# Input projections of the last mixers as three single-pass products over half weight items

## The reference

```
h = rms_norm_2(x, norm1_g) * (1.0 + sc1) + sh1
hc = rms_norm_2(ctx, norm1_g) * (1.0 + csc1) + csh1
mq, mk, mv, mo, mg, gq, gk, gv, gr, glr = split(z)        # z = h @ w_in and hc @ w_in
mq, mk = split(silu(short_conv(concat(mq, mk), conv_w)))
gates = mg + gate_b ; alpha = glr @ lr_w2 + alpha_b
```

## Time and profile before

| what | value |
|---|---|
| runs | 1684.7, 1689.92, 1689.48 us; median 1689.48 |
| profiled execution | 1686.99 us, of which the span is 1685.3 us |
| TensorE | 1622.6 us busy, 96% of the span |
| VectorE | 1082.2 us, 64% |
| ScalarE | 683.4 us, 41% |
| GpSimd | 32.5 us, 2% |
| TensorE's clock | full but for a few tenths of the span |
| bytes moved | 293.56 MB, mean 174 GB/s |

### The profile page before, as it was taken

How to read it: one execution, slowest core, us unless ns; L and a number is a source line. 1 busy time by engine, 2 the same in 40 slices (tenths; PEclk the granted TensorE clock), 3 DMA queues, 4 the chain that set the end, 5 groups by cost and what they waited for, 6 DMA issues and landing times.

```text
span 1685.3 us, 27871 instructions
## 1 busy us (share of the span) xinstructions
PE 1622.6 (96%) x10342; PEld 1399.5 (83%) x10342; DVE 1082.2 (64%) x1928; ACT 683.4 (41%) x972; POOL 32.5 (2%) x80
## 2 busy tenths in 40 slices
PE   7999898999999999999899999999999999999997
PEld 6676567789999456678899999999999888888885
DVE  6992221346543536736549999898884777777776
ACT  4225112244432233222344565554555444444442
POOL 2002000000000000100000000000000000000000
PEclk9999899999999999999999999999999999999999
DMA  6352934435555222031428887755556777777773
GB/s 259 124 197 100 397 110 179 168 119 186 190 176 170 74 75 100 1 111 40 175 88 230 221 230 225 216 162 160 152 162 209 230 231 230 232 232 232 233 232 109
DMA packets 92382, 293.56 MB, mean 174 GB/s; under 512 B 10256, under 2 KB 43152, under 8 KB 77584
## 3 DMA queue, kind: packets, MB, share of 16 engines
q1 hardware_dynamic: 92160, 292.21, 54.1%
q10 hardware_dynamic: 144, 0.26, 0.0%
HBM read 274.60 MB, written 17.83 MB: 174 GB/s over the span
## 4 chain that ended last, share of the span: by engine, by line
PE 89%; DVE 6%; DMA 3%; ACT 1%; issue 1%; SPq 0%; DVEq 0%; ACTq 0%
PE ps L380 89%; DMA ring<-in_w_mod 1%; DVE big L1254 1%; DVE split_ring L1744 1%; DVE big L1163 1%; DMA ring<-in_peer_u 1%; DVE x L1879 0%; DMA kept_acts<-acts 0%; DVE big L1793 0%; DVE big L1797 0%; DVE big L1795 0%; DVE hh L1464 0%; DMA ring<-in_peer_v 0%; DMA x<-in_x 0%; DVE big L1652 0%
## 5 line engine op out<-in xcount | busy, mean ns | idle before, releaser
L380 PE MATMUL ps<-split_hh,split_ring 128*128 128x256 f32 x3072 | 378.2, 284 | 2.6 <-DVE split_ring L1744 2.3
L380 PEld LDWEIGHTS ps<-split_hh,split_ring 128*128 128x128 f32 x3072 | 370.9, 192 | 3.9 <-DVE split_ring L1744 1.7
L380 PE MATMUL ps<-split_ring 128*128 128x512 f32 (+1 forms) x2048 | 362.5, 340 | 2.6 <-DVE split_ring L1744 2.6
L380 PEld LDWEIGHTS ps<-split_ring 128*128 128x128 f32 x2048 | 313.8, 188 | 51.2 <-DVE split_ring L1744 3.3
L1744 DVE TENSOR_TENSOR split_ring<-ring,split_ring 128x1024 fp32r<-128x1024 f32 x256 | 312.0, 1221 | 48.8 <-ACT split_ring L2239 46.8
L380 PE MATMUL ps<-hh,ring 128*128 128x256 f32 (+1 forms) x816 | 206.8, 414 | 7.9 <-DVE hh L1186 4.3
L2246 ACT ACTIVATE split_ring<-ring 128x1024 fp32r<-128x1024 f32 x128 | 135.9, 1062 | 185.1 <-DMA ring<-in_peer_v 185.1
L380 PEld LDWEIGHTS ps<-hh,ring 128*128 128x128 f32 x816 | 156.1, 192 | 57.2 <-issue 37.7
L2239 ACT ACTIVATE split_ring<-ring 128x1024 fp32r<-128x1024 f32 x128 | 135.3, 1057 | 76.6 <-DMA ring<-in_peer_u 76.4
L380 PE MATMUL ps<-split_ffn_h,split_ffn_w 128*128 128x256 f32 x1056 | 130.3, 287 | 3.5 <-ACT split_ffn_h L2100 3.5
L380 PEld LDWEIGHTS ps<-split_ffn_h,split_ffn_w 128*128 128x128 f32 x1056 | 129.2, 194 | 4.6 <-issue 3.9
(11 more groups left out here) (296 smaller groups left out, 1615.9 us busy)
## 6 DMA issues: line engine op xcount, KB each, us to landing
ring<-in_peer_u SPq DMA_DIRECT2D x128, 512.0 KB, 4.0
ring<-in_peer_v SPq DMA_DIRECT2D x128, 512.0 KB, 3.7
ring<-in_w_mod SPq DMA_DIRECT2D x24, 1024.0 KB, 5.1
ring<-in_ffn_in SPq DMA_DIRECT2D x22, 1024.0 KB, 4.9
ring<-kept_acts SPq DMA_DIRECT2D x128, 128.0 KB, 3.4
ring<-in_ffn_out SPq DMA_DIRECT2D x11, 1024.0 KB, 4.9
ring<-in_w_out SPq DMA_DIRECT2D x8, 1024.0 KB, 9.3
ring<-in_peer_wq SPq DMA_DIRECT2D x8, 1024.0 KB, 5.9
```

What stands on the lines that cost most here:

```text
L380: return nc.tensor.matmul(out, lhsT, rhs, start=start, stop=stop, skip_group_check=True)
```

## The change

- Gates, `mk`, `mq`, `mv`, `gk`, `gq`, `gv`, `mo` and `gr` are computed as three single-pass products of rounded values and remainders. `three` does it for 256 columns and 8 tiles (24 matmuls); a product over both token sets is now two such groups, 48 matmuls; a value block is 24 matmuls of 512 columns.
- The two token sets are split into high and low once (`ctx_high`, `ctx_low`, `lat_high`, `lat_low`): ScalarE copies, VectorE subtracts, in place of the plain tensors.
- Their weights come as 29 "half items" of 512 KB: gates 0, mk 1 to 4, mq 5 to 8, mv 9 to 12, gk 13 and 14, gq 15 and 16, gv 17 to 20, mo 21 to 24, gr 25 to 28. Five ring slots hold one half item each, in the order `HALF_SLOTS`: the rounded copy goes to the slot's other half, the remainder over the raw weights. The sixth slot holds `ctx_high`. SyncE loads half n + 5 when the product that used half n is made; for gk, mk and the gates that is one half, for mq, gq, mo and gr both halves of the product, for mv and gv all four after the fourth block.
- ScalarE's copies (`half_high`) and VectorE's subtractions (`half_low`) are placed by hand in the two engines' orders. The loads of the output weights now come behind the last half item.
- The context part of the gates is computed before `lat_sum`'s matmuls and the context part of key 0 behind them; the latent parts follow when the latent tokens are ready.
- The convolution of the last two queries moves behind the four `alpha` rows, and the gates' output tile `out_g` gets another place.
- Normaliser: four fp32 products with the tile of ones become one, over the sum of the head's four tiles, which GpSimd adds in three steps per head and direction (`weight_sums`, `weights_summed`).

```diff
+HALF_SLOTS = (1, 2, 4, 3, 0)
...
+        weight_sums = std.rearrange("p h (d t) -> p h d t", d=2)
...
+        def half_tiles(n):
+            s = HALF_SLOTS[n % 5]
+            return half_slots[:, 2 * s, :], split_slots[:, 2 * s + 1, :], split_slots[:, 2 * s, :]
...
+            def half_split(n, nk=KD):
+                pe.wait_ge(flag("halves_split"), n + 1)
+                return (t.rearrange("p (k c) -> p k c", k=nk) for t in half_tiles(n)[1:])
...
+            def three(out, n, high, low, first_, arriving_=None):
+                w_high_, w_low_ = half_split(n)
+                for t, (w, rhs) in enumerate(((w_high_, high), (w_low_, high), (w_high_, low))):
+                    for k in range(KD):
...
+                        last = mm(out, w[:, k, :], rhs[:, k, :], first_ and t == 0 and k == 0, t == 2 and k == KD - 1)
+                return last
...
-            bank = ahead_of(0)
+            sum_bank, gate_bank = ahead_of(0), ahead_of(1)
+            gates = next_half("gates", 0, 0)
+            pe.wait_ge(flag("ctx_split"), 1)
+            three(gate_bank[:, 0:T], gates, ctx_high, ctx_low, True)
             for i in range(4):
-                last = part_of_sum(bank, "lat_sum", i)
-            whole_sum(bank, "lat_sum", last)
...
+                last = part_of_sum(sum_bank, "lat_sum", i)
+            whole_sum(sum_bank, "lat_sum", last)
+            key_bank = ahead_of(1)
+            first_key = next_half("w2_mk", 0, 0)
+            three(key_bank[:, 0:T], first_key, ctx_high, ctx_low, True)
...
+            three(gate_bank[:, T:], gates, lat_high, lat_low, False, ("lat_high_ready", "lat_split")).then_inc(made, 1)
+            release_half(gates)
...
+            def project_lat(name, i, upper=0):
+                bank = begin((name, i), "act", upper=upper)
+                ws = [next_half("w2_" + name, i, m) for m in range(2)]
+                for m in range(2):
+                    last = three(bank[:, m * T:(m + 1) * T], ws[m], lat_high, lat_low, m == 0)
                 last.then_inc(made, 1)
+                release_half(*ws)
...
                     for half in range(2):
+                        if half:
+                            pe.wait_ge(flag("weights_summed"), 2 * hd + dr + 1)
+                            last = mm(bank[:, T:], ones, weight_sums[:, hd % 2, dr, :])
+                            continue
...
+                    for m, (name, i, part) in enumerate(halves_):
+                        slot = HALF_SLOTS[m % 5]
+                        before = released[max(k for k in range(gap) if k % RING == slot)] if m < 5 else halves_released[m - 5]
+                        sp.wait_ge(made, before)
+                        sp.dma_start(half_tiles(m)[0], d[name][i][:, 1024 * part:1024 * part + 1024])\
+                            .then_inc(flag(f"half_in_slot{slot}"), 16)
...
+            def half_low(*ns):
+                for n in ns:
+                    raw_, high, low = half_tiles(n)
+                    s.wait("halves_high", n + 1)
+                    v.tensor_tensor(low, raw_, high.bitcast(F32), ALU.subtract).then_inc(flag("halves_split"), 1)
...
             last.then_inc(flag("gla_diffs_ready"), 1)
+            half_low(13)
...
             decays(0)
             decayed(0)
+            half_low(14, 15)
             for hd in range(MH):
                 if hd + 1 < MH:
                     decays(hd + 1)
                     decayed(hd + 1)
+                if hd == 0:
+                    half_low(16, 17, 18, 19, 20)
+                if hd == 3:
+                    half_low(22, 23)
                 quotient(hd)
                 if hd == 0:
                     decayed_keys_and_queries()
+                if hd == 1:
+                    half_low(21)
...
+                    act.wait_ge(flag(f"half_in_slot{HALF_SLOTS[n % 5]}"), 16 * (n // 5 + 1))
+                    a_(high, raw_, ACT.Copy).then_inc(flag("halves_high"), 1)
...
+                    link(g.tensor_tensor(total_, e[:, dr, 0, :], e[:, dr, 1, :], ALU.add))
+                    link(g.tensor_tensor(total_, total_, e[:, dr, whole_, :], ALU.add))
+                    g.tensor_tensor(total_[:, half_], total_[:, half_], e[:, dr, 5 - whole_, half_], ALU.add)\
+                        .then_inc(flag("weights_summed"), 1)
```

166 lines of the change are left out of this document (126 added, 40 removed).

## The result

The changed kernel takes 1691.58 us (median of 20 runs, 1685.97 to 1695.71), the kernel before 1687.78 in the same rounds. The ratio is 1.0025, 95% interval 1.0015 to 1.0036: 4.2 us slower by the ratio, between 2.5 and 6.1 (3.8 between the medians). The forecast was 2 us less.

The account below looks back on a forecast made before the run. TensorE bounds the kernel (busy 96%), with VectorE's slack nil before 682. Of 38 us saved, most is lost to waits and the clock: -4.1 to +0.4, middle 2 us faster, 1685.0 against 1686.99, median 1686; range 1666 to 1696.

Parts of the forecast that it names:

- step 5: TensorE's clock falls after new waits before gk 1 and inside gq: 0 to 3.4 us more.
- The loop: Row products of head 1 wait behind gk 1, quotient of head 0 behind half 20; VectorE 5.6 us later.
- step 6: After the quotient of head 0: decays of head 2 at 686.1 to 689.5, gr 1 ready 761.9 to 766.4.
- Step 2: Keys to value blocks: value block 0 starts at 600.3, second block ends at 610.9; gain 11.6 us.
- Steps 4 and 5: Scores of head 0 to its quotient: start at 673.5, or 676.9 with the full clock charge; 667.92 before.
- What TensorE saves: Shorter products: 8 us on chunks, 8 on latent projections, 13 on value blocks, 9 on normalisers; sum 38 us.
- all 38 us arrive: Rival: TensorE's whole saving reaches the kernel's time, 1648 us; chance 3 in 100.
- Step 1, head: Start of the stage: gates made at 563.4 with half of key 0 done; gain 2.5 us.
- Step 3: Second value block's copy to scores of head 0: scores at 644.0, gain 10.6; 14 us of TensorE's saving lost.
- GpSimd's adds: 24 two-input adds at 0.7 us each, 4 us a head; nothing waits below 1.5 us an add.
- The slower rival: GpSimd's adds hold VectorE's remainders, each of two loop links up to 4 us longer; 1695 us, chance 0.20.
- The faster rival: TensorE keeps more of its gain, as hand-overs may be over-priced by 1 us a link; 1676 us, chance 0.33.

Follow-up runs that it names:

- e1: Changed kernel with the old normaliser, four fp32 products on TensorE and no GpSimd adds: ratio 1.0034 to the kernel before.
- e12: Changed kernel with only half 13 split earlier, ahead of VectorE's wait for the logarithm: ratio 1.0032 to the kernel before.
- e4: Changed kernel with half 20 split behind the quotient of head 0 and the decayed keys and queries: ratio 1.0015 to the kernel before.
- e7: Changed kernel with products that nobody reads filling four of TensorE's waits: ratio 1.0026 to the kernel before.
- e3: Changed kernel with half 13 split ahead of the logarithm wait, halves 14 and 15 ahead of the decays of head 0: ratio 0.9948 to the kernel before.
- e5: e3 with half 16 split right behind the scores of head 0: ratio 0.9936 to the kernel before.
- e6: e5 with half 20 split between the quotient of head 0 and the decayed keys: ratio 0.9921 to the kernel before.
- e8: e5 with ScalarE's five GLA exponentials moved behind those of the decays of head 1: ratio 0.9924 to the kernel before.

## Why the prediction was wrong

The step that failed is step 5, the charge for TensorE's clock. The loop and its waits were where the prediction put them; this term was too small. It charged two places, gk 1 and the second half of gq, with 0 to 3.4 us and took the middle (of a range that had grown to 4.5 us at the end of the stage, without a reason given, so 2.2 us there). The rows show 3.2 us at those two places, 0.9 at the gates and 1.5 at `mo 1`, 5.6 in all. The forecast had the stage end 1.9 us earlier, and it ended 3.9 later. Of that miss of 5.8 us the clock is 3.4, and of these the 1.5 at `mo 1` are chance (step 6). The rest is small terms of steps 2, 4 and 6. With the charge taken whole the same sum gives 0.4 us slower.

"Slower" had a chance of 0.22, but for causes that the runs refute.

- **What TensorE saves** (38 us): busy time in the stage fell by 25.7. Most of the difference is records at half the clock: against the same groups at the full clock those at 632, 647, 668, 693 and 746 last about 10 us longer. The products were priced well (24 passes of 256 columns take 2.88 us, as taken). A value block takes 5.44 (24 x 0.227), not 5.3. That all 38 us arrive would have been 1649 us, not 1648.
- **Step 1, head:** gates at 564.4, not 563.4. The high passes were done when the remainder was ready (562.28), as forecast; the eight records behind it then took 1.87 us, to 564.15, where they take 0.96 at the full clock (granted 0.50 at 559 to 565).
- **Step 2:** value block 0 at 601.6 (600.3), its second copy at 612.8 (610.9). With step 1 these make the scores of head 0 end at 645.7, not 644.0: 1.7 us short.
- **Step 3:** right in kind. TensorE waited for half 13 until 632.5 and for half 14 until 647.1, 11.3 us of idle where I had 13.9; gk 0 itself was 2.2 us longer, at the half clock. TensorE's idle in the whole stage is 32 us.
- **Steps 4 and 5.** The quotient was put at 673.5, or 676.9 with the clock's full charge, and the forecast took the middle. It came at 678.9: 1.7 from the steps ahead; 1.7 and 1.5 from gk 1 and the second half of gq, whose 16 records took 3.79 and 3.62 us in place of 2.1; 0.5 left over. Of these some 0.4 are halves 14 and 16, each 0.2 longer beside the adds than I had priced; yet e1 has no adds and its quotient at the same place, so even they are not shown to cost anything. The charge was thus paid nearly whole. The granted clock was 0.50 also at 632 to 636 and 693 to 697, but both lie beside the path: behind gk 0 TensorE waited again, and from decays of head 2 to the quotient of head 1 it is 8.9 us, as before. A forecast that has written down a charge for a place where the engine will stand has to take it whole.
- **Step 6:** decays of head 2 at 691.4 (686.1 to 689.5), `gr 1` done at 769.9 (761.9 to 766.4). Beside the 5.4 us carried on from the quotient, the last stretch, from the quotient of head 3 at 738.4, took 2 us more than its walk. 1.5 of them are the clock again, at `mo 1`, behind a wait for the quotient (rows below). The 24 records from 745.72 last to 750.18, 4.46 us, and those from 754.66 to 757.63, 2.97. e12 lost the same there (3.11 us for the 16, behind 1.31 us of wait); e4 and e7 did not (2.18, behind 1.37 and 1.42). What decides is not shown, and the sum could not have had it but as a chance. 0.6 more came between the decays of head 2 and the quotient of head 3; for them I found no term. The output weights were no issue.
```profile
744.69 1.09 PE L423 MATMUL ps<-big 64*64 64x128 f32 x16 [1.59 <-DVE big L1772]
745.72 3.22 PE L423 MATMUL ps<-split_head,split_ring 128*128 128x256 f32 x16
...
754.66 2.17 PE L423 MATMUL ps<-split_head,split_ring 128*128 128x256 f32 x16
```
- **GpSimd's adds:** taken at 0.7 us each. Alone they take 0.73 (256 columns) and 0.46 (128), beside a remainder 1.59 and 1.32. The Trainium skill ("GPSIMD Engine Reference", section 3.1, "Elementwise", not Key points as the prediction has it) gives 4497 ns for 2048 elements. The estimate worked out from it, 0.56 us for 256 columns, was too low beside 0.73. The Trainium skill ("GPSIMD Engine Reference", Key points) has the two engines contend where VectorE's instruction reads two SBUF operands; by that rule the rows of GpSimd and VectorE agree (1.59 and 3.11 us). What e1 adds is that none of it reached the quotient, and that the kernel is no faster without it (1.0034). The slower rival, with up to 4 us a link, is refuted as the cause; 0.8 and 1.6 are its size for the two groups of halves.
- **The faster rival** (hand-overs priced too high) did not come true: half 20 came 6.4 us behind gq, as priced. e3 comes near its number by another way, 9 us below the kernel before where the rival had 11: its 13 us against the changed kernel are hand-overs that this order had put into a loop.

Why the change made it slower can be said in one line: it takes 26 us of work from TensorE and ties what follows to VectorE's queue, where halves 14 and 15 stand behind the scores of head 0 and ahead of what TensorE needs for the rows of head 1, and halves 16 to 20 ahead of the quotient. Splitting 14 and 15 ahead of that loop returns 13 us; the later edits that helped (e5, e6, e8) return 2 or 3 each, within the intervals. How much of the loop is the clock is not separated by a run: e7 filled the waits and gained 1.1 us on the path, with gk 1 still at the half clock.

## What to carry to other kernels

When an edit adds helper work to another engine's in-order queue, find the cycle first: which engine waits for the helper, and what does the queue behind the helper wait for in turn. A helper inside such a cycle can cost far more than its own length (moving halves 14 and 15, two splits of 1.2 us, brought the decays of head 1 forward by 11.5), one outside costs nothing (half 13), so place the first kind in idle time ahead of the cycle, even where its result is wanted much later. And measure both parts of a double edit alone: the adds were worth 6 us by themselves and nothing beside the halves.

## What the runs showed of the hardware

- GpSimd's two-input add and VectorE's two-input subtraction slow each other down: the add from 0.73 to 1.59 us (256 columns), two subtractions of 1024 columns from 2.35 to 3.11, four from 4.62 to 6.19. The 0.76 us that the two grow by is close to one add alone. Whether one engine waits for the other or both slow down, no run here shows. VectorE's rows that read an accumulation bank beside an add keep their length: 0.42 us at 700.77 in the changed trace, and the add at 700.85 takes 0.73.
- After waits of 4.76, 6.54, 6.60 and 6.87 us TensorE's next stretch was granted half the clock. With the waits filled it stayed at 1.00 behind an idle of 0.46 us and was 0.50 behind one of 2.13 us. Behind a wait of 1.59 us at 744.69 it fell to 0.61 and 0.54 (746 to 750), and in e7, behind 1.42 us at the same place, it stayed at 1.00.
